# A gated linear recurrence in 3 blocks of 96 tokens instead of 128, 128 and 32, with the masked scores of a block gathered in one matrix

## What is computed

```
q = silu(q);  fg = lb + (1 - lb) * sigmoid(f);  k = 1 - fg;  b = cumsum(log fg)
a[t, u] = sum_d q[t, d] * k[u, d] * exp(b[t, d] - b[u, d])      for u <= t in the block
o[t]    = sum_u a[t, u] * v[u]  +  (q[t] * exp(b[t])) @ S
S_new   = exp(b_last) * S + sum_u (k[u] * exp(b_last - b[u])) v[u]^T
o       = rms_norm(o) * silu(g);   y = o @ w_out
```

## Time and profile before

| | |
|---|---|
| runs, device time | 2974.03, 2974.07, 2976.63 us (median 2974.07) |
| the profiled execution: span from first to last instruction | 2973.6 us |
| PE busy | 2823.9 us, 95% |
| PEld busy | 2771.7 us, 93% |
| DVE busy | 1797.9 us, 60% |
| ACT busy | 1254.5 us, 42% |
| POOL busy | 454.2 us, 15% |
| the recurrence, from the first to the last scores | 79.6 to 671.1 us, 15 positions |

### The profile page before, as it was taken

How to read it: one execution, slowest core, us unless ns; L and a number is a source line. 1 busy time by engine, 2 the same in 40 slices (tenths; PEclk the granted TensorE clock), 3 DMA queues, 4 the chain that set the end, 5 groups by cost and what they waited for, 6 DMA issues and landing times.

```text
span 2973.6 us, 57264 instructions
## 1 busy us (share of the span) xinstructions
PE 2823.9 (95%) x20626; PEld 2771.7 (93%) x20626; DVE 1797.9 (60%) x2994; ACT 1254.5 (42%) x2054; POOL 454.2 (15%) x856
## 2 busy tenths in 40 slices
PE   6999999998899999999999888889799999999997
PEld 6999999998799999999999778789799999999997
DVE  6566566664766664566665743445766644667755
ACT  5444444442444443344433443433544433444432
POOL 3111111000232210122200200000322200222200
PEclk9999999998899999999999889999899999999998
DMA  5333333333344455545455331224354455544553
GB/s 197 112 117 116 105 111 99 109 119 103 118 154 165 165 160 166 167 163 166 163 162 166 113 102 64 70 82 166 107 168 161 165 162 166 168 162 163 162 168 115
DMA packets 124258, 413.61 MB, mean 139 GB/s; under 512 B 14032, under 2 KB 22384, under 8 KB 124176
## 3 DMA queue, kind: packets, MB, share of 16 engines
q1 hardware_dynamic: 116064, 406.37, 42.4%
q10 hardware_dynamic: 7056, 3.21, 0.4%
q0 software_dynamic: 1056, 2.92, 0.3%
HBM read 406.97 MB, written 5.48 MB: 139 GB/s over the span
## 4 chain that ended last, share of the span: by engine, by line
PE 87%; DVE 8%; ACT 2%; issue 2%; DMA 1%; POOL 0%; SPq 0%; DVEq 0%; ACTq 0%; POOLq 0%
PE bank L219 27%; PE bank L221 26%; PE bank L220 26%; PE bank L546 2%; PE bank L574 2%; DVE X L777 1%; DVE h_lo L782 1%; DVE Y L502 1%; DVE Y L773 1%; DVE Y L501 1%; DMA raw<-in_w_hi_in 1%; PE bank L534 0%; PE bank L551 0%; PE bank L1210 0%; POOL ssx L757 0%
## 5 line engine op out<-in xcount | busy, mean ns | idle before, releaser
L219 PE MATMUL bank<-h_hi,w_hi 128*128 128x288 f32 (+1 forms) x4208 | 1288.8, 306 | 79.2 <-DVE h_lo L782 46.8
L220 PE MATMUL bank<-h_lo,w_hi 128*128 128x288 f32 (+1 forms) x4208 | 1266.1, 301 | 0.0
L221 PE MATMUL bank<-h_hi,w_lo 128*128 128x288 f32 (+1 forms) x4208 | 1262.2, 300 | 0.0
L213 DVE TENSOR_TENSOR w_lo<-raw,w_hi 128x1024 fp32r<-128x1024 f32 (+2 forms) x786 | 941.5, 1208 | 497.5 <-ACT w_hi L206 496.5
L206 ACT ACTIVATE w_hi<-raw 128x1024 fp32r<-128x1024 f32 (+2 forms) x786 | 807.8, 1036 | 967.7 <-PE bank L221 952.2
L219 PEld LDWEIGHTS bank<-h_hi,w_hi 128*128 128x128 f32 x4208 | 805.4, 191 | 94.1 <-issue 50.2
L220 PEld LDWEIGHTS bank<-h_lo,w_hi 128*128 128x128 f32 x4208 | 807.2, 192 | 1.9
L221 PEld LDWEIGHTS bank<-h_hi,w_lo 128*128 128x128 f32 x4208 | 808.7, 192 | 0.4
L219 PE MATMUL bank<-g_hi,w_hi 128*128 128x288 f32 x1408 | 416.9, 296 | 0.0
L220 PE MATMUL bank<-g_lo,w_hi 128*128 128x288 f32 x1408 | 415.6, 295 | 0.0
L221 PE MATMUL bank<-g_hi,w_lo 128*128 128x288 f32 x1408 | 414.2, 294 | 0.0
(11 more groups left out here) (231 smaller groups left out, 2395.2 us busy)
## 6 DMA issues: line engine op xcount, KB each, us to landing
raw<-in_w_fi SPq DMA_DIRECT2D x352, 512.0 KB, 4.0
raw<-in_w_hi_in SPq DMA_DIRECT2D x128, 512.0 KB, 3.9
raw<-in_w_fo SPq DMA_DIRECT2D x128, 512.0 KB, 3.5
raw<-in_w_fo SPq DMA_DIRECT2D x64, 384.0 KB, 3.2
raw<-in_w_ho SPq DMA_DIRECT2D x32, 512.0 KB, 4.2
raw<-in_w_mo SPq DMA_DIRECT2D x32, 512.0 KB, 3.9
raw<-in_w_down SPq DMA_DIRECT2D x18, 512.0 KB, 4.4
raw<-in_w_ukv SPq DMA_DIRECT2D x16, 512.0 KB, 3.8
```

What stands on the lines that cost most here:

```text
L213: dve.tensor_tensor(w_lo[:, ch.slot, 0:n], raw[:, ch.slot, 0:n], w_hi[:, ch.slot, 0:n].bitcast(F32), ALU.subtract).then_inc(lo_done, 1)
L219: pe.matmul(out, w_hi[:, ch.slot, w], rhs_hi, start=start, stop=False)
L220: pe.matmul(out, w_hi[:, ch.slot, w], rhs_lo, start=False, stop=False)
L221: return pe.matmul(out, w_lo[:, ch.slot, w], rhs_hi, start=False, stop=stop)
```

## The change

The 288 tokens are cut in three blocks of 96: 0 to 95, 96 to 191, and 192 to 287, whose first 64 tokens are the end of the prompt and whose last 32 are the sample. Five near levels (1 to 16 tokens) stay; the far pairs of a block are two rectangles, tokens 0 to 31 with 32 to 63 (`FAR1`, in all three blocks) and tokens 0 to 63 with 64 to 95 (`FAR2`, in the first two). The level of one token and the diagonal share a matmul of 144 columns with the bare keys as weights. The scores of a block lie in one PSUM bank, one bank to a block (`scores3`). DVE then gathers the valid entries of a block in one matrix `att` of 96 x 96: two copies for the far rectangles, then six predicated copies with a drain before each. One matmul per block applies `att`. There is one more state update and one more state (`s_mid` has two). Constants (`carry`, zeroes in `lev` and `ktok`) are set once at the start.

The core of the diff:

```diff
+        BL = 96
+        NB = T // BL
+        NEAR = 5
-        BLOCKS = [(0, P), (P, P), (TP, TS)]
+        ENDS = [(0, BL), (BL, BL), (2 * BL, TP - 2 * BL), (TP, TS)]
...
-                act.activation(ktok[:, 0:2, :], TR[:, 0:2 * P], ACT.Copy)
-                act.activation(ktok[0:TS, 2, :], TR[0:TS, 2 * P:3 * P], ACT.Copy).then_inc(S["k_tok"], 1)
+                act.activation(ktok[0:BL, 0:2, :], TR[0:BL, 0:2 * P], ACT.Copy)
+                act.activation(ktok[0:64, 2, :], TR[0:64, 2 * P:3 * P], ACT.Copy)
+                act.activation(ktok[64:BL, 3, :], TR[64:BL, 2 * P:3 * P], ACT.Copy).then_inc(S["k_tok"], 1)
...
-                act.activation(vtok[:, 0:2, :], TR[:, 0:2 * P], ACT.Copy)
-                act.activation(vtok[0:TS, 2, :], TR[0:TS, 2 * P:3 * P], ACT.Copy).then_inc(S["v_tok"], 1)
+                act.activation(vtok[0:BL, :, :], TR[0:BL, 0:3 * P], ACT.Copy).then_inc(S["v_tok"], 1)
...
-                for n, (b0, bn) in enumerate(BLOCKS):
+                for n, (b0, bn) in enumerate(ENDS):
                     e = act.activation(HG.EE[:, b0:b0 + bn], HG.B[:, b0:b0 + bn], ACT.Exp, scale=-1.0,
...
-                act.activation(HG.Z[:, 0:5 * T], HG.Z[:, 0:5 * T], ACT.Exp)
-                v = HG.Z[:, 5 * T:7 * T].rearrange("p (l t) -> p l t", l=2)[:, :, 0:TP]
-                act.activation(v, v, ACT.Exp).then_inc(S["diffs_exp"], 1)
+                act.activation(HG.Z[:, 0:HG.ZN], HG.Z[:, 0:HG.ZN], ACT.Exp).then_inc(S["diffs_exp"], 1)
...
-                for n, lv in enumerate((LVA, LVB)):
-                    dve.tensor_tensor(lev[:, n, :], lv[:, 0:LEVELS * 64], level_mask, ALU.mult)
-                dve.tensor_tensor(diag[:, 0:TP].rearrange("p (n t) -> p n t", n=2), DG[:, 0:TP].rearrange("p (n t) -> p n t", n=2),
-                                  ident[:].unsqueeze(1).to_broadcast([P, 2, P]), ALU.mult)
-                dve.tensor_tensor(diag[0:TS, TP:T], DG[0:TS, TP:T], ident[0:TS, 0:TS], ALU.mult)
-                dve.tensor_tensor(lev_s[:], DG[0:TS, T:T + 5 * 16].rearrange("p (l t) -> p l t", l=5),
-                                  level_mask_f[0:TS, 0:5, 0:16], ALU.mult).then_inc(S["att_ready"], 1)
+                dve.tensor_copy(att[0:32, :, 32:64], scores3[0:32, :, FAR1:FAR1 + 32])
+                dve.tensor_copy(att[0:64, 0:2, 64:BL], scores3[0:64, 0:2, FAR2:FAR2 + 32])
+                dve.drain()
+                dve.copy_predicated(att, ident[0:BL, 0:BL].bitcast(U32).unsqueeze(1).to_broadcast([BL, NB, BL]),
+                                    scores3[0:BL, :, 0:BL])
+                for l in range(NEAR):
+                    m, c = 2 ** l, BL + l * (BL // 2)
+                    dve.drain()
+                    mask = level_mask_f[0:BL, l, 0:BL // 2].bitcast(U32).rearrange("p (s m) -> p s m", m=m)
+                    z = dve.copy_predicated(block_halves(att, m)[1],
+                                            mask.unsqueeze(1).to_broadcast([BL, NB, BL // (2 * m), m]),
+                                            scores3[0:BL, :, c:c + BL // 2].rearrange("p b (s m) -> p b s m", m=m))
+                z.then_inc(S["att_ready"], 1)
...
-                dve.wait_ge(S["mid_state"], t + 1)
-                dve.scalar_tensor_tensor(out=s_new[:, 0, :], in0=s_mid[:], scalar=HG.EB[:, TP - 1:TP],
-                                         in1=SU[:, P:2 * P], op0=ALU.mult, op1=ALU.add).then_inc(S["states"], 1)
+                dve.wait_ge(S["first_state"], t + 1)
+                dve.scalar_tensor_tensor(out=s_mid[:, 1, :], in0=s_mid[:, 0, :], scalar=HG.EB[:, 2 * BL - 1:2 * BL],
+                                         in1=SU[:, P:2 * P], op0=ALU.mult, op1=ALU.add).then_inc(S["second_state"], 1)
+                dve.wait_ge(S["second_state"], t + 1)
+                dve.scalar_tensor_tensor(out=s_new[:, 0, :], in0=s_mid[:, 1, :], scalar=HG.EB[:, TP - 1:TP],
+                                         in1=SU[:, 2 * P:3 * P], op0=ALU.mult, op1=ALU.add).then_inc(S["states"], 1)
...
-                for n, (b0, bn) in enumerate(BLOCKS):
-                    su = pe.matmul(SU[:, n * P:(n + 1) * P], ktok[0:bn, n, :], vtok[0:bn, n, :], start=True, stop=True)
+                for n in range(NB + 1):
+                    su = pe.matmul(SU[:, n * P:(n + 1) * P], ktok[0:BL, n, :], vtok[0:BL, min(n, NB - 1), :], start=True, stop=True)
...
+                for n in range(NB):
+                    c = n * BL
+                    pe.matmul(OV[:, c:c + BL], vtok[0:BL, n, :], att[:, n, :], start=True, stop=(n == 0), skip_group_check=True)
+                    if n == 1:
+                        pe.matmul(OV[:, c:c + BL], s_mid[:, 0, :], qb[:, c:c + BL], start=False, stop=True, skip_group_check=True)
+                    if n == 2:
+                        pe.matmul(OV[:, c:TP], s_mid[:, 1, :], qb[:, c:TP], start=False, stop=False, skip_group_check=True)
+                        ov = pe.matmul(OV[:, TP:T], s_old[:], qb[:, TP:T], start=False, stop=True, skip_group_check=True)
...
+                for n in range(NB):
+                    out, c = scores3[0:BL, n, :], n * BL
+                    pe.matmul(out[:, 0:BL + BL // 2], key[:, c:c + BL], qz[:, n, :], start=True, stop=True)
+                    for l in range(1, NEAR):
+                        z = z_level(l)[:, c:c + BL]
+                        at = BL + l * (BL // 2)
+                        pe.matmul(out[:, at:at + BL // 2], z, halves(z, 2 ** l)[1], start=True, stop=True)
+                    z = HG.Z5 + n * 64
+                    lv = pe.matmul(out[:, FAR1:FAR1 + 32], HG.Z[:, z:z + BL], HG.Z[:, z + 32:z + 64], start=True, stop=True)
+                    if n < NB - 1:
+                        z = HG.Z6 + n * BL
+                        pe.matmul(out[:, FAR2:FAR2 + 32], HG.Z[:, z:z + BL], HG.Z[:, z + 64:z + BL], start=True, stop=True)
```

More of the change, by code:

```diff
@@ L18 @@
 F32R = mybir.dt.float32r
+U32 = mybir.dt.uint32
 ALU = mybir.AluOpType
@@ L106, in sem @@
             return ctx.enter_context(nc.semaphore(name))
-        psum = [ctx.enter_context(nc.psum_tensor(f"bank{n}", [P, 512], F32)) for n in range(8)]
+        psum = [ctx.enter_context(nc.psum_tensor(f"bank{n}", [P, 512], F32)) for n in range(5)]
+        scores3 = ctx.enter_context(nc.psum_tensor("bank5", [P, 3, 512], F32))
+        psum += [scores3[:, n, :] for n in range(3)]
         raw = sb("raw", [P, RING, UNITS * P])
@@ L312, in trunk_program @@
         hg = ctx.enter_context(ExitStack())
+        BL = 96
+        NB = T // BL
+        NEAR = 5
+        DIAG, FAR1, FAR2 = 0, BL + NEAR * (BL // 2), BL + NEAR * (BL // 2) + 32
+        assert NB * BL == T and TP % BL == 64 and TS == 32
         class HG:
@@ L316, in trunk_program @@
             Z = base[:, 0:LEVELS * T]
+            Z0 = Z[:, 0:T // 2]
+            Z1 = T // 2
+            Z5 = Z1 + (NEAR - 1) * T
+            Z6 = Z5 + NB * 64
+            ZN = Z6 + (NB - 1) * BL
             o = LEVELS * T
@@ L322, in trunk_program @@
             EE = base[:, o + 8 * T:o + 9 * T]
-        assert 16 * T >= (LEVELS + 9) * T
+        assert 16 * T >= (LEVELS + 9) * T and HG.ZN <= LEVELS * T
+        qz = row_tiles[:, 4:6, :].rearrange("p r t -> p (r t)")[:, 0:NB * (BL + BL // 2)].rearrange("p (b n) -> p b n", b=NB)
+        query, odd_q = qz[:, :, 0:BL], qz[:, :, BL:BL + BL // 2]
+        att = lev[0:BL, 0, 0:T].rearrange("p (b t) -> p b t", b=NB)
         on = yt[:, 0, :]
@@ L339, in halves, with block_halves, z_level, z_far1 @@
             return v[:, :, 0, :], v[:, :, 1, :]
[L341 to L347, removed]
+        def block_halves(ap, m):
+            v = ap.rearrange("p b (s two m) -> p b s two m", two=2, m=m)
+            return v[:, :, :, 0, :], v[:, :, :, 1, :]
+        def z_level(l):
+            return HG.Z[:, HG.Z1 + (l - 1) * T:HG.Z1 + l * T]
+        def z_far1():
+            z = HG.Z[:, HG.Z5:HG.Z6].rearrange("p (b t) -> p b t", b=NB)
+            return z[:, :, 0:32], z[:, :, 32:64]
+        def z_far2():
+            z = HG.Z[:, HG.Z6:HG.ZN].rearrange("p (b t) -> p b t", b=NB - 1)
+            return z[:, :, 0:64], z[:, :, 64:BL]
+        def by_block(ap):
+            return ap.rearrange("p (b t) -> p b t", b=NB)
+        def ref_col(m):
+            v = HG.B[:, 0:T].rearrange("p (b two m) -> p b two m", two=2, m=m)
+            return v[:, :, 0, m - 1:m].to_broadcast([P, T // (2 * m), m])
         def on_position(split, eng, j, k):
@@ L562, in hgrn_pe @@
                 pe.wait_ge(S["v_tok"], r + 1)
-                for n, (b0, bn) in enumerate(BLOCKS):
-                    tr = pe.transpose(TR[0:bn, n * P:(n + 1) * P], ke[:, b0:b0 + bn], ident[:])
+                for n in range(NB):
+                    tr = pe.transpose(TR[0:BL, n * P:(n + 1) * P], ke[:, n * BL:(n + 1) * BL], ident[:])
                 tr.then_inc(S["k_turned"], 1)
@@ L1365, in first @@
                     split_lo(dve, IN, 0, k)
+                dve.memset(lev[:], 0.0)
+                dve.memset(ktok[:], 0.0).then_inc(S["zeroed"], 1)
```

(5 more changed lines are left out.)

95 lines of the change are left out of this document (47 added, 48 removed).

## The result

The changed kernel takes 2869.64 us (median of 4 runs, 2868.34 to 2869.97), the kernel before 2975.35 us (4 runs, 2974.03 to 2976.95): a ratio of 0.9641, 95% interval 0.9629 to 0.9654. The forecast was 2887 us, the range 2872 to 2908. In the profiled executions the span fell from 2973.6 to 2867.6 us, by 106.0, where the prediction's sum had 87.0.

What follows compares the result with a forecast made beforehand. PE was taken as the bound. Stages -69.6, waits -4.9, last masks +1.0 and clock -13.5 sum to -87.0 us, from the profiled 2973.6 to 2886.6, plus 0.5 for the median: 2887 us, range 2872 to 2908.

Steps and rivals of the forecast that it cites:

- hidden chain: States, decays, exponents or ACT come forward as the application shrinks; half its gain lost, 2919 us; chance 0.06.
- 0.086 by the line: PE's step price with 96 columns of weights, on a line through 0.034 us (32 columns) and 0.112 (128).
- the three stages on PE: Per head: application -4.0 us, scores -0.5, updates +0.15; over 16 heads -69.6.
- the last masks: DVE's masks in the last head, with nothing beside them to hide behind: +1.0 us once.
- the clock: PE's nine falls to 1.2 GHz after the thin application all go: -13.5 us.
- a change of the shape of the weights costs about 0.1: PE's recurrence: 0.1 us per change of weight shape, four in the application adding 0.4.
- The low end: 2872 us: no change of shape costs anything (11 us) and the wait at the scores vanishes (4 us).
- the wait shrinks from 0.63 to 0.3: PE's wait at the scores for DVE's products: -0.35 us, 14 times, -4.9 in all.
- Rival 1: PE's clock falls stay or move behind the scores, now on 96 of 128 columns: 2900 us; chance 0.19.
- Masks: DVE's new mask set takes 2.7 us, hidden beside PE's work except in the last head; may last 5.0.
- Rival 4: PE's weights of 96 cannot load beside the preceding matmul, so each step costs 0.2 us: 3013 us, slower; chance 0.04.
- the sign would have turned: PE's recurrence: from 0.19 us a step on, in place of the assumed 0.11, the gain becomes a loss.

Runs made afterwards that it cites:

- experiments 1 and 4: 1: gathering as in the change, but the old blocks of 128, 128 and 32, 2895.82 us; 4: kernel before without the sample block's five level matmuls, 2937.51 us.
- 3: The changed kernel with each block's gathered matrix applied in slices of 16 columns, 42 steps in place of 12: 2956.84 us.
- experiments 9 and 10: Kernel before with GpSimd's rescales held back behind DVE's products: the third and fourth in 9, 2959.61 us; all four in 10, 2951.91 us (one run).
- experiment 8: The changed kernel with the five predicated copies of the near levels done three times over: 2931.05 us.
- experiment 6: The changed kernel with one more matmul on 96 rows, to unread columns, ahead of each block's application: 2877.49 us (one run).

## Why the prediction was right or wrong

**Right: the bound, and what carries the gain.** PE was and is the bound, PE's stages shrank by at least what the steps are worth, and no hidden chain came forward (the exponents still leave DVE idle 3.02 us, the masks have 1.7 us of slack). The step on 96 columns of weights, 0.086 by the line, measures 0.085, and that of 144 columns 0.12 for 0.12: the second block takes 213.67 - 212.41 = 1.26 us, of which its two steps of 144 up to 212.71 take 0.30 with the block's first gap, and its twelve others 12 x 0.08.

The forecast's sum of 87.0 us and the measured 106.0 differ by 19.0: the three stages on PE gave 84.9 instead of 69.6 (15.3), the wait 8.8 instead of 4.9 (3.9), the last masks cost 0.4 more, and the clock with the rest gave 0.2 more.

**Wrong: "a change of the shape of the weights costs about 0.1".** It was read from changes to and from 32 rows and carried over to 96. It holds for 32 (0.155 each), not for 96, where it is nothing. It was 0.4 of the application's 1.75, 0.2 of the updates' 1.1 and 0.15 of the scores' 3.75: 12 us over 16 heads, the largest part of the miss. The low end did allow for this. It did not allow for steps cheaper than the 0.112 that stood for all with 128 columns of weights: the updates' eight take 0.81 / 8 = 0.101 each, and the application's four of 64 and 32 columns 0.10. That and rounding are the other 3.3 us of the stages, and it is why the result lies below the range.

**Half wrong: "the wait shrinks from 0.63 to 0.3".** In five positions of fourteen it does just that: the wait is 0.27, and the stage lost 4.06 - 3.70 = 0.36 us for a forecast of 0.35. In the other nine it lost 0.78. The sum over DVE's products counted columns and instructions at 0.22 start to start, but three of the fourteen took 0.84, beside GpSimd's rescales, and in those nine positions the third of them kept the pace of the others. That is 9 x 0.42 = 3.8 us more; the low end, which let the wait vanish, had room for it. In the five the slow products stand on both sides of the difference and cancel. They stood in DVE's timeline of before; the 0.22 was read from a pair of other instructions, the subtractions for the exponents, and taken for all.

**Right: the clock.** The falls in the positions went, all nine, and 13.7 us remain beside the forecast's 13.5. (Nine falls of 1.5 are 13.5; the last head's tail, 3.4 us longer at the lower level, takes an estimated 1.5 back, so some 1.7 have another source.) That they need a thin application, or a wait, is shown by experiments 1 and 4 (without it, none) and 3 (thin steps put back, on other rows and in other numbers, in every position). It isn't all: with the application untouched experiments 9 and 10 have four and two falls in place of nine, so something else in a position counts too, and that stays open. The Trainium skill's rule that ties a fall to an idle gap ("TensorE: Matmul & The Clock Gate", section "Why this matters for your kernels") fails here, since PE was busy for 4.60 of 4.60 us before one; but the traces give it something too, as waits of 2.1 to 3.0 us brought falls back in experiment 8, and in the changed kernel the clock falls within the last head's wait of 3.33 us. Rival 1 is refuted: in the positions the scores, 3.57 us of 96 columns of weights, are never followed by a fall.

**Masks:** 3.2 us for 2.7. The predicated copies of 144 columns take 2.21 / 5 = 0.44 each with their drains, the one of 288 takes 0.56 to the start of the next, so most of the price is in the instruction. It hides as the prediction said. In the last head it shows in full, 3.33 where I had 2.90; +1.4 instead of +1.0.

**Rival 4** is refuted: steps of 96 rows follow at 0.11 us and less, far from the 0.19 at which the sign would have turned. On the Trainium skill's rule that a weight load overlaps only where its row group differs ("TensorE: Matmul & The Clock Gate", section "Part 3: Packing small matmuls — row/col tiling"): by it the six steps on the same 96 rows in experiment 6 should stand apart; they take 0.112 each, and in experiment 3 weight loads and matmuls are both busy for the whole of 4.60 us.

## What to carry to other kernels

Cost a small fp32 matmul by its step (here 0.10 to 0.11 us with 128 columns of weights and 0.085 with 96, almost whatever it moves up to 96 columns), so that fewer and wider steps win, and check both the changes to 32 rows and what a thin stretch does to the clock behind it. When a wait hangs on a row of equal instructions, list them one by one: a few may be three times as long, beside another engine's work, and a shift of 0.35 us gave 0.36 in some positions and 0.78 in others. A change in two parts may be worth less than nothing in one of them: these blocks need the gathering.

## What was not expected of the hardware

- Matmuls on 96 rows follow those on 128 without a gap; changes to and from 32 rows cost 0.155 us each.
- The clock falls behind or within a stretch of thin steps during which PE never idles: 42 steps of mostly 16 columns in 4.61 us, in all positions; 38 steps of mostly 64 and 128 columns in 4.36 us, in none. With the same 48 steps in 5.77 us it fell in nine, four or two positions, depending on when GpSimd's rescales ran.
- Where DVE and GpSimd work at once, either can be the one that loses: a product of 0.3 us lasts 0.92 beside a rescale, and a rescale of 0.8 to 0.9 us lasts 5.4 to 6.0 when DVE's `w_lo` splits follow each other. The order of the starts doesn't tell which: the rescale started 0.06 us before the product at 111.26 and at 243.05 alike, and lost only the second time. Since nobody was waiting for the rescale, the second way was the cheap one, and holding the rescales back was worth 16 us (the third and fourth) and 24 us (all four, one run) in the kernel before, fewer falls of the clock included.
